# Attention, output projection, second norm and router as one pipeline over row tiles, with the output weights split on ScalarE and VectorE

## The reference

```python
h = rms_norm(x, norm_mix_g[l]) * (1.0 + sc1) + sh1
proj = h @ w_in[l]
gm_out = gmlp_mixer(proj[..., :o1], ...)
mla_out = mla_mixer(proj[..., o1:o2], proj[..., o2:o3], proj[..., o3:], cos, sin, ...)
mixed = jnp.concatenate([rms_norm(gm_out, out_norm_g[l, :GM_WIDTH]),
                         rms_norm(mla_out, out_norm_g[l, GM_WIDTH:])], axis=-1)
x = x + g1 * (mixed @ w_out[l])
h = rms_norm(x, norm_ffn_g[l]) * (1.0 + sc2) + sh2
x = x + g2 * moe_ffn(h, w_router[l], router_bias[l], ...)
```

## Time and profile before

| | us |
|---|---|
| median of three runs | 1121.76 |
| lowest, highest | 1113.04, 1123.85 |
| the profiled execution | 1113.93 |
| its span on the core | 1112.0 |
| TensorE, VectorE, ScalarE, GpSimd busy | 971.8, 905.2, 602.3, 278.4 |

### The profile page before, as it was taken

One profiled execution on the slowest core, in us unless ns is written; L12 is line 12 of the kernel. 1 busy time (PEld: TensorE's weight loads), 2 busy tenths in 40 slices (PEclk: granted clock), 3 DMA queues, 4 the chain that ended last, 5 costly groups with the idle time before them and its releaser, 6 DMA issues.

```text
span 1112.0 us, 14197 instructions
## 1 busy us (share of the span) xinstructions
PE 971.8 (87%) x4335; PEld 745.7 (67%) x4336; DVE 905.2 (81%) x1280; ACT 602.3 (54%) x948; POOL 278.4 (25%) x186
## 2 busy tenths in 40 slices
PE   3797899898999979898999988989897999898895
PEld 1354375586788657677777777777676777677684
DVE  3687877754566878998999999999998899898894
ACT  1123153466113046676777766667675767676672
POOL 1004105130000202323234232332323232324232
PEclk9899899889999989999999999999999999999897
DMA  9976402200027278999999999999999999999973
GB/s 310 393 280 232 151 1 76 104 2 1 19 89 276 67 294 268 374 318 339 325 340 359 344 333 339 326 337 333 327 349 327 309 333 356 351 327 350 341 257 59
DMA packets 86232, 286.79 MB, mean 258 GB/s; under 512 B 18052, under 2 KB 18564, under 8 KB 77112
## 3 DMA queue, kind: packets, MB, share of 16 engines
q1 hardware_dynamic: 64240, 248.03, 61.1%
q0 software_dynamic: 19056, 36.89, 13.2%
q10 hardware_dynamic: 2904, 1.48, 0.5%
HBM read 283.04 MB, written 37.88 MB: 289 GB/s over the span
## 4 chain that ended last, share of the span: by engine, by line
DMA 49%; PE 29%; DVE 11%; issue 6%; ACT 1%; SPq 1%; POOL 1%; POOLq 0%; DVEq 0%; ACTq 0%
DMA out<-oute,src_tab 44%; PE bank L633 5%; PE bank L574 4%; PE bank L575 4%; PE bank L576 4%; DMA xe<-h_rows,src_tab 3%; DMA ada_w<-in_w_ada 2%; DVE ada_acc L1234 2%; PE bank L787 2%; PE bank L708 2%; PE bank L725 1%; DVE gu_low L1466 1%; DVE q_sb L1313 1%; PE bank L804 1%; PE bank L716 1%
## 5 line engine op out<-in xcount | busy, mean ns | idle before, releaser
L1466 DVE TENSOR_TENSOR gu_low<-w_gu,gu_high 128x1024 fp32r<-128x1024 f32 x256 | 301.4, 1218 | 10.6 <-ACT gu_high L1103 5.4
L1103 ACT CAST gu_high<-w_gu 128x1024 fp32r<-128x1024 f32 x256 | 256.6, 1055 | 62.8 <-PE bank L576 57.2
L530 POOL DMA_INDIRECT out<-oute,src_tab x64 | 128.9, 2015 | 465.0 <-DMA out<-oute,src_tab 357.5
L574 PE MATMUL bank<-gu_high,xeT_high 128*128 128x512 f32 x512 | 208.1, 406 | 2.8 <-DVE xeT_low L1466 2.6
L576 PE MATMUL bank<-gu_high,xeT_low 128*128 128x512 f32 x512 | 202.1, 395 | 0.0
L575 PE MATMUL bank<-gu_low,xeT_high 128*128 128x512 f32 x512 | 201.8, 394 | 0.0
L1466 DVE TENSOR_TENSOR d_low<-w_d,d_high 128x1024 fp32r<-128x1024 f32 x128 | 150.4, 1216 | 0.0
L1109 ACT CAST d_high<-w_d 128x1024 fp32r<-128x1024 f32 x128 | 128.1, 1053 | 18.0 <-PE bank L576 18.0
L820 PE MATMUL bank<-ident,xe 128*128 128x128 f32 x512 | 73.5, 288 | 60.3 <-DMA xe<-h_rows,src_tab 58.4
L820 PEld LDWEIGHTS bank<-ident,xe 128*128 128x128 f32 x512 | 64.5, 194 | 81.3 <-issue 77.6
L574 PE MATMUL bank<-d_high,hwT_high 128*128 128x512 f32 x256 | 112.3, 439 | 6.7 <-DVE hwT_low L1466 6.5
(11 more groups left out here) (278 smaller groups left out, 1291.6 us busy)
## 6 DMA issues: line engine op xcount, KB each, us to landing
w_gu<-in_w_exp_gate SPq DMA_DIRECT2D x128, 512.0 KB
w_gu<-in_w_exp_up SPq DMA_DIRECT2D x128, 512.0 KB
w_d<-in_w_exp_down SPq DMA_DIRECT2D x64, 1024.0 KB, 8.6
ada_w<-in_w_ada SPq DMA_DIRECT2D x12, 2048.0 KB, 11.9
w_out_sb<-in_w_out SPq DMA_DIRECT2D x2, 2048.0 KB, 7.2
w_lat_sb<-in_w_in SPq DMA_DIRECT2D x1, 2688.0 KB, 21.9
x_sb<-in_x SPq DMA_DIRECT2D x1, 2048.0 KB, 24.2
w_v_sb<-in_w_in SPq DMA_DIRECT2D x1, 2048.0 KB, 10.3
```

The costliest lines, as they stand in the source:

```text
L530: pool.indirect_dma_start(out_rows, bass.IndirectOffsetOnAxis(ap=rows, axis=0), oute[i][:], None, bounds_check=last_row, oob_is_err=False, ...
L574: pe.matmul(dst, xh, wh, start=start, stop=False)
L1103: act.copy(gu_high[half][:, m], w_gu[half][i][:, m]).then_inc(gu_high_ok[half], 1)
L1466: return dve.tensor_tensor(low, whole, high.bitcast(F32), ALU.subtract)
```

## The change

- **Modulation.** x is loaded first. For blocks 0 to 3 TensorE sums chunks 0 to 3 and VectorE chunks 4 to 7. The gain G1 is made in two halves. The transfers of the small parameters on ScalarE's queue are issued behind silu(c).
- **Output weights.** GpSimd's split is gone. ScalarE makes the high part of each chunk with the gain `on_g` in it (`wout_high`), four chunks ahead of the gelu of u and four in the first tile's heads; VectorE makes the low part (`wout_lower`) in those heads.
- **Order.** Tiles go from 3 to 0 (TILES), in attention and everything up to the router. Between two heads each engine has a piece of the tile before (p - 1) or of the one before that (p - 2), set by `between_heads` on the engine.
- **Banks.** Scores have two banks (NSB = 2) and run two heads ahead, transposes two, the weighted values one, the projection two, and one bank, T_BANK, serves all other transposes and the router in turn.
- **Norms.** The square roots of the output norms and of the second norm are made on VectorE (`rsqrt_mean`: a start value and three steps, twelve small operations), not on ScalarE.
- **Router and behind.** One copy of logits for each tile; the sigmoid stays one. The last tile's rows are stored by GpSimd. The shared expert takes its tiles in the new order, its first gate product stands ahead of the last tile's h2 transposes. ScalarE converts the first expert's gate and up weights of half 1 behind the routing, since the tile lies elsewhere in SBUF; some other tiles move too. The loop over experts is as it was.

```diff
+                pe.wait_ge(ld_ada[j], 16)
+                for c in range(ADA_HALF):
+                    last = pe.matmul(bank[j % 2][:], cbc[:, c, :], ada_w[j][:, c, :], start=(c == 0), stop=False)
+                last.then_inc(ada_pe, 1)
+                pe.matmul(bank[j % 2][:], ident[0:ADA, j:j + 1].to_broadcast([ADA, P]), b_ada[0:ADA, :], start=False, stop=False)
...
-            for n, i in enumerate((2, 3, 0, 1)):
-                if n % 2 == 0:
-                    pool.wait_ge(ld_wout[i // 2], 16)
-                if n == 2:
-                    pool.wait_ge(qkT_tr, 4 * T)
-                part_of = slice(i * (C // 4), (i + 1) * (C // 4))
-                pool.tensor_copy(w_out_high[i][:], w_out[:, part_of]).then_inc(wout_high_ok, 1)
-                pool.wait_ge(wout_high_ok, n + 1)
-                pool.tensor_tensor(w_out_low[:, part_of], w_out[:, part_of], w_out_high[i][:].bitcast(F32), ALU.subtract).then_inc(wout_ok, 1)
...
+            def mixed_transposes(p, half):
+                if half == 0:
+                    pe.wait_ge(mix_ok, p + 1)
+                    if p:
+                        pe.wait_ge(mixT_low_ok, 2 * p)
+                    if p >= 2:
+                        pe.wait_ge(logit_ok, p - 1)
+                else:
+                    pe.wait_ge(mixT_low_ok, 2 * p + 1)
+                for n, c in enumerate(W_ORDER[half * 4:half * 4 + 4]):
+                    last = pe.transpose(bank[T_BANK][:, n * P:(n + 1) * P], mixed[:, TILES[p], c::C], ident[:])
...
+            def out_projection(p, g0, g1):
+                for g in range(g0, g1):
+                    m, n = divmod(g, C)
+                    c = W_ORDER[n]
+                    cols = slice(m * BANK, (m + 1) * BANK)
+                    pe.wait_ge(mixT_low_ok, 2 * p + 1 + n // (C // 2))
+                    if p == 0 and m == 0:
+                        pe.wait_ge(wout_ok, n + 1)
...
+            OUT_CUTS = (0, 3, 6, 9, 12, 2 * C)
+
+            def between_heads(p, hd):
+                if p >= 1:
+                    if hd in (1, 2):
+                        mixed_transposes(p - 1, hd - 1)
+                    if hd >= 3:
+                        out_projection(p - 1, OUT_CUTS[hd - 3], OUT_CUTS[hd - 2])
+                if p >= 2:
+                    if hd in (4, 5):
+                        h2_transposes(p - 2, hd - 4)
+                    if hd == 6:
+                        router(p - 2)
+
+            for i in range(NSB):
...
+            def between_heads(p, hd):
+                if p == 0 and hd < C // 2:
+                    wout_high(C // 2 + hd)
+                if p >= 1 and hd in (1, 2):
+                    mixed_high(p - 1, hd - 1)
+                if p >= 2:
+                    if hd in (4, 5):
+                        h2T_copy(p - 2, hd - 4)
...
-            gate_up_high_of(0, (None, 0))
-            gate_up_high_of(1, (None, 0))
             shared_silu(0)
             shared_silu(1)
+            gate_up_high_of(0, (None, 0))
             shared_hT_copy(0)
             shared_silu(2)
             shared_hT_copy(1)
             shared_silu(3)
             shared_hT_copy(2)
             act.wait_ge(src_ok, 1)
+            gate_up_high_of(1, (None, 0))
             rows_high_of((None, 0))
             shared_hT_copy(3)
             act.wait_ge(shw_ok, T)
...
+            def rsqrt_mean(col, n):
+
+                k = col.shape[1]
+                y, sq, half = root[:, 0:k], root_sq[:, 0:k], root_half[:, 0:k]
+                link(dve.tensor_scalar(col, col, 1.0 / n, EPS, ALU.mult, ALU.add))
+                dve.tensor_scalar(half, col, -0.5, None, ALU.mult)
+                link(dve.tensor_scalar(y.bitcast(I32), col.bitcast(I32), -0.5, float(0x5F375A86), ALU.mult, ALU.add))
+                for step in range(3):
+                    link(dve.tensor_tensor(sq, y, y, ALU.mult))
+                    link(dve.tensor_tensor(sq, sq, half, ALU.mult))
+                    link(dve.scalar_tensor_tensor(y if step < 2 else col, sq, 1.5, y, ALU.add, ALU.mult))
+
+            def square_sum(p, s):
...
+            def outputs(p):
+                t = TILES[p]
+                dve.wait_ge(av_mm, (p + 1) * H)
                 link(dve.reciprocal(den[:, t, :], den[:, t, :]))
-                dve.tensor_tensor(mixed[:, t, GW:D].rearrange("p (h d) -> p h d", h=H), bank[6 + t % 2][:].rearrange("p (h d) -> p h d", h=H),
+                dve.tensor_tensor(mixed[:, t, GW:D].rearrange("p (h d) -> p h d", h=H), bank[O_BANK][:].rearrange("p (h d) -> p h d", h=H),
                                   den[:, t, :].unsqueeze(2).to_broadcast([P, H, VD]), ALU.mult).then_inc(o_ok, 1)
-                dve.wait_ge(o_ok, t + 1)
+                dve.wait_ge(o_ok, p + 1)
+                link(square_sum(p, 1))
+                rsqrt_mean(oss[:, t, :], GW)
                 for s in range(2):
-                    last = dve.tensor_tensor_reduce(osq[:, s * GW:(s + 1) * GW], mixed[:, t, s * GW:(s + 1) * GW], mixed[:, t, s * GW:(s + 1) * GW], 1.0, 0.0, ALU.mult, ALU.add, oss[:, t, s:s + 1])
-                if t < T - 1:
-                    link(last)
-                else:
-                    last.then_inc(oss_ok, 1)
-
-            dve.wait_ge(gate_ok, GG)
-            for i in range(NI):
...
+            def between_heads(p, hd):
+                if p == 0:
+                    wout_lower(hd)
+                if p >= 1:
+                    if hd == 0:
+                        outputs(p - 1)
+                    if hd in (1, 2):
+                        mixed_low(p - 1, hd - 1)
+                if p == 1 and hd == 3:
+                    second_gain()
+                if p >= 2:
+                    if hd == 2:
+                        residual(p - 2)
+                    if hd == 3:
+                        norm2(p - 2)
+                if hd == 6:
+                    link(square_sum(p, 0))
+
+            dve.wait_ge(gate_ok, GG)
+            row_max(0)
+            for i in range(NI):
+                if i + 1 < NI:
+                    row_max(i + 1)
+                between_heads(*divmod(i, H))
...
```

403 lines of the change are left out of this document (213 added, 190 removed).

## The result

| | us | first scores | key transpose | between them |
|---|---|---|---|---|
| before | 1122.80 (1113.04 to 1124.77) | 219.15 | 353.51 | 134.4 |
| after | 1165.56 (1162.69 to 1172.07) | 212.97 | 404.04 | 191.1 |

The times are medians of four runs each; the two right-hand markers are rows of TensorE's timeline in the profiled executions. The ratio is 1.041, 95% interval 1.033 to 1.048: the change makes the kernel slower by 4%.

What follows compares the result with a forecast made beforehand. TensorE, nearly always busy, was taken to bound the part before the router; DMA-heavy experts would shift as a block. 1112.0 - 3 - 4.5 + 45.6 + 7 + 3 = 1160.1 us of span, 1162 with 1.9 more; range 1114 to 1190.

Steps and rivals of the forecast that it cites:

- The first norm: Front modulation, sums shared by TensorE and VectorE: normalised rows start earlier, 3 us saved, bounds 1 and 4.3.
- The weights: Output weights without GpSimd's split: k transposes no longer wait for VectorE, first scores 4.5 us earlier.
- The walk: Pipeline followed head by head with its waits: 180.0 us from first scores to key transpose against 134.4, 45.6 lost.
- 5.3 at `residual()`: Third tile: TensorE waits 5.3 us where VectorE's residual() stands ahead of a maximum.
- Twice 2.3 for the mixed transposes: Second tile: round trips through one shared bank delay the next exponential, TensorE waits 2.3 us, twice.
- the 3.5 at `norm2()`: Third tile: TensorE waits 3.5 us at VectorE's norm2().
- The tail and the clock: Tail behind the head loop: outputs, projection halves, norm, router and shared products, keys transposed 48.0 us after the loop.
- The wait of 5.1 for `norm2()` of the third tile: Tail, between first half of the projection and h2 transposes: TensorE waits 5.1 us for VectorE's norm2().
- 12 us, less the 5: Clock lowered behind idle gaps: 12 us, less 5 that slow first heads cost before, so 7, bounds 0 and 25.
- Rival 2: Clock stays at 0.50 through short heads into projection groups, which double, some 33 us: 1200 us; chance 0.08.
- Behind the keys: Start of the experts: ScalarE converts gate weights later, delaying the shared hidden product 3 us, bounds 0 and 3.5.
- Rival 1: Pipeline waits fall under work, if VectorE's pieces stay under about 2.5 us: 1097, or 1104 without the clock; chance 0.13.

Runs made afterwards that it cites:

- e4: The changed kernel without the three steps of the inverse square root, ten small VectorE operations fewer per call: 1154.19 us, ratio 1.039.
- e5: The changed kernel with VectorE's pieces cut to at most 3.3 us and projection groups moved beside them, same work: 1148.47 us, ratio 1.030.
- e6: The changed kernel with unread identity transposes as fillers in TensorE's waits in the last three tiles: 1162.38 us, ratio 1.043.
- e10: The kernel of e5 with unread identity transposes in seven idle places of TensorE behind the last head: 1141.98 us, ratio 1.025.
- e7: The changed kernel with the second half of the first expert's gate weights converted ahead of the shared expert's copies again: 1162.77 us, ratio 1.043.
- e2: The kernel before with the new modulation and output-weight split but no pipeline: 1119.49 us against 1114.39, ratio 1.006.

## Why the prediction was right, step by step

Predicted were 1162.0 us, measured 1165.56.

**The first norm.** -3 us, measured -3.02 at 46.05. **The weights.** VectorE's multiplications are short again and the k transposes do not wait. Both terms together were -7.5 at the first scores and came to -6.2: the wait for the modulation sums that come by DMA gave 1.1 of the 3 us back (the first sum at 114.60 instead of 116.48).

**The walk.** Each tile of the walk ends with the projection groups behind its last head. By these ends it gave 22.8, 34.0, 39.0 and 36.2 us, 132.0 in all; the trace has 21.2, 38.1, 40.0 and 36.2, or 135.4 (212.97 to 348.4). The waits it named are there: 4.1 at the second head of the second tile (3.65), 5.3 at `residual()` (4.57 and 4.75). e4 and e5 confirm the mechanism: shorter pieces gave 12.8 us, the same pieces beside groups 17.1.

That the sum is so near is in part luck, since two errors cancel. The waits were put too high: 42.4 us in the second to fourth tile (8.7, 16.3, 17.4), measured 29.5 (6.7, 10.3, 12.5). Twice 2.3 for the mixed transposes were twice 1.53, and the 3.5 at `norm2()` is 0.24 in the third tile. Part of that is half clock, at which TensorE's own work covers more of a wait: the three groups ahead of `norm2()`'s wait took 4.0 us, not 2.1. In e6, at 0.91, the wait is 1.50, still not 3.5. And TensorE's own work was put too low: 67.2 us in these tiles (25.1, 23.3, 18.8), measured 84.8, at a clock of 0.75 to 0.82.

**The tail and the clock.** "The keys are transposed 48.0 us after the loop"; it was 55.6 (348.4 to 404.04). The two halves of the projection, router and shared products took 9.9 us longer than their terms, and the round trips of the mixed transposes 5.3 us instead of 3.2. The wait of 5.1 for `norm2()` of the third tile did not come: it lay under the slower projection (in e10, near the full clock, it is 2.42).

So the term that was mis-sized is the clock, "12 us, less the 5": 7 for the whole stage. TensorE's work took 17.6 us more in the tiles and some 10 in the tail, and the waits that were put too high hid most of it. The stage took 191.1 us against 180.0 + 7; the 4.1 us between them and 1.3 of the front are the 5.3 us by which the span exceeds the sum (1165.4 against 1160.1), to rounding. Not all of the slower work could be won back: fillers alone gave 4.3 us in the second tile and 7.2 in the tail, nothing in the third and fourth.

Rival 2, half clock from the short heads on through all projection groups, did not come: the clock was 0.75 to 0.82. The rule of the Trainium skill behind it (TensorE: Matmul & The Clock Gate, on the second failure mode) describes what the traces show in kind, a clock that goes up and down behind small idle pieces.

**Behind the keys.** 3 us, measured 3.1 between keys and first scatter; e7 takes 2.1 of it back.

**Rival 1**, waits under work, asked for pieces under about 2.5 us. In e5 most are (the longest is 3.1), and it is 1148, not 1097 to 1104. My price for it was wrong: two more round trips through one bank stay, and the tail is longer than the end of the old stages. What is left of the pipeline's cost, 169.0 us in e10 against 134.4, is some 16 us more of waits (25.7 against 9.5 us, rows of 0.2 us and more from the first scores on) and 18 us more of TensorE's time, some 9 of it fillers (80 of 0.11 us). No run splits the rest, and none holds the full clock through a pipeline without paying for fillers.

## What to carry to other kernels

When stages are made into a pipeline on engines that work in order, count at each place what the waiting engine has queued behind its last finished item, not how much work there is in all: here it was one head's scores, 0.4 to 1.5 us, against pieces of 3 to 6. Put the filling work (projection groups) exactly beside the long pieces, and the chain that remains behind the last item is the price to look at first. And read a saving at the next stage's start and again at its end: in e2 6.2 us saved in front were lost in the heads behind it, at half clock.
